# A Mamba-style decoder step: clamping the decay exponents on ScalarE in place of a mask matmul, and a first chunk without a carried state

## The chip, the cores and the metric

The kernel runs on one core of one Trainium2 chip. The metric is the device time of one execution in microseconds (us); the document gives the median of several runs. One core has a matrix engine (TensorE, PE in the profile; its weight loads are listed apart as PEld), a vector engine (VectorE, DVE), an activation engine (ScalarE, ACT), GpSimd (POOL) and a queue that issues most DMAs (SyncE, SP). The engines run their own instruction streams and meet only at semaphores.

## The reference, cut to what matters

One decoder layer is computed for a prompt of 512 tokens and for 8 sample tokens: a combined projection, a state-space (SSD) branch and a pooling branch, cross-attention, an MLP and norms. The change touches only the chunked SSD scan over the prompt, with 4 chunks of 128 tokens, 32 heads in 4 groups, head size 64 and state size 128:

```python
cs = jnp.cumsum(dt * A, axis=2)                       # per chunk and head; A < 0, dt > 0
seg = cs[:, :, :, None] - cs[:, :, None, :]           # l (out token) minus s (in token)
lmat = jnp.exp(jnp.where(causal, seg, -jnp.inf))      # causal: l >= s
cb = jnp.einsum('bclgn,bcsgn->bclsg', Cm, Bm)
y_diag = jnp.einsum('bclsgk,bcsgkp->bclgkp', cb[..., None] * lmat, xdt)
chunk_states = jnp.einsum('bclgn,bclgkp->bcgkpn', Bm, xdt * decay_to_end[..., None])
def step(s, inp):
    dec, st = inp
    return s * dec[..., None, None] + st, s
s_fin, s_prev = lax.scan(step, s0, (chunk_decay, chunk_states))   # s0 = 0 for the prompt
y_off = jnp.einsum('bclgn,bcgkpn->bclgkp', Cm, s_prev) * jnp.exp(cs)[..., None]
y = y_diag + y_off                                    # then + d_skip * xs
```

Since dt is positive and A negative, cs falls along a chunk, so seg is not positive wherever the mask keeps it.

## The kernel before, in words

Every large projection is a run of calls `gemm(t)` over tiles t of 128 output columns: 48 matmuls each (8 slices of the contraction, three products of split float32 operands, two halves of 260 tokens), all on line 376. For each tile ScalarE makes `w_hi` (line 354), VectorE makes `w_lo` (line 361), and the result stays in one of two PSUM slots until it is evacuated.

The SSD scan is woven into these projections. It has 16 steps s = 1 to 16, four chunks c (0 to 3) times four groups gr (0 to 3). TensorE's stream for it is written out in full. For each step it issues:

- `step_a`: the product of B and C (line 1651), a transpose of B (line 1652), and `rows_of_cs` for heads 0 to 3, then the semaphore `cb_ready`.
- tiles of the projection: in chunks 0 and 1 a whole tile of 48 matmuls (none for s = 1), in chunks 2 and 3 half a tile, 24 matmuls.
- `step_b`: it waits for `exp_a` (ScalarE) and `x_prep` (VectorE), then issues `rows_of_cs` for heads 4 to 7, the product of C with the carried state (line 1660) and the new chunk state (line 1661), then `off_ready`.
- another whole tile (chunks 0 and 1) or the second half tile (chunks 2 and 3).
- `step_c`: it waits for `m_ready` (VectorE), then issues the products of the eight decay matrices with the inputs (line 1667), then `y_mm`.

`rows_of_cs` writes a PSUM bank of 4 heads by 128 tokens with two matmuls of 512 columns: line 1644 multiplies a bfloat16 identity by a mask that holds 0 or -1e30, and line 1646 adds the cumulative sums, spread over the partitions.

ScalarE runs two loops of two iterations (lines 745 to 767) with four groups each. For each step it copies `b_tok` and then turns the bank into `decay[:, 0:4]` with four activations (`decays`, line 732: Exp of the row plus a per-partition bias `ncs`, the negated sum), which sets `exp_a`; after `off_ready` it does the same for heads 4 to 7 (`exp_b`). Between these it serves the projection tiles (`split_hi`, line 354, and a tanh or a copy).

VectorE's loops are `prep` (lines 1123 and 1124, the second sets `x_prep`), `weights_a` (line 1129 multiplies C B by the triangle `triu` into `cbm`, line 1131 multiplies `decay[:, 0:4]` by `cbm`), `carry` (line 1136 scales the state's output, lines 1137 and 1139 renew the state, line 1141 multiplies `decay[:, 4:8]` by `cbm` and sets `m_ready`), and `finish_y` (lines 1146 and 1148). In chunks 0 and 1 two projection tiles are served in between (lines 361 and 1153), in chunks 2 and 3 one. GpSimd zeroes the state (line 502), builds the constants at the start (lines 471 to 488) and computes the skip term of each step (line 507).

## Time and profile before

| | us |
|---|---|
| median of three runs | 1327.97 |
| lowest and highest run | 1327.3 and 1332.85 |
| the profiled execution, its time | 1328.24 |
| its span, first to last instruction | 1326.5 |
| TensorE matmul busy in it | 1266.1 (95%) |
| VectorE busy | 760.0 (57%) |
| ScalarE busy | 451.2 (34%) |
| GpSimd busy | 163.9 (12%) |

The span is shorter than the device time by 1.7 us, which lies outside the first and last instruction. All positions in time below are microseconds from the start of the span. The scan's 16 steps lie between 198.5 and 411.7. Busy shares are means over stages with different limits, so what a change is worth must be read from its own stage. The records of matmuls overlap because they are pipelined; the distance between the starts of successive records tells what one costs, not its duration. The mean granted TensorE clock was 0.978 of full speed.

### The profile page before, as it was taken

How to read it: one execution, taken by the hardware profiler on the slowest of the kernel's cores; microseconds unless marked ns; L12 is line 12 of the kernel's file. 1: busy time of each engine (PE TensorE's matmuls, PEld its weight loads, DVE VectorE, ACT ScalarE, POOL GpSimd, SP SyncE). 2: the span in 40 equal slices, each digit the busy share in tenths (PEclk: the TensorE clock that was granted, in tenths of full speed). 3: DMA queues.
4: the chain of work that ended last, by engine and by line, in shares of the span. 5: the costliest groups of instructions: out<-in, count | busy, mean ns of one | idle time of the engine just before them, and what ended most of it. 6: DMA issues, size and time to landing. Idle time of an engine off the chain costs nothing.

```text
span 1326.5 us, 23554 instructions
## 1 busy us (share of the span) xinstructions
PE 1266.1 (95%) x9799; PEld 1190.4 (90%) x9799; DVE 760.0 (57%) x1494; ACT 451.2 (34%) x752; POOL 163.9 (12%) x194
## 2 busy tenths in 40 slices
PE   6999999999998999699999998999999999999996
PEld 5999998998887988699999985459999999999996
DVE  5677866666776656753444457323645765743433
ACT  4444423333332235432245223223431331322422
POOL 1000003000112733200010000001112222200000
PEclk7999999999998999899999997999999999999998
DMA  6423222222124563042234639401645556433211
GB/s 220 120 64 94 73 65 82 73 65 64 33 80 130 144 163 93 32 161 96 88 104 168 214 108 366 161 0 64 206 138 179 176 178 190 144 112 96 96 64 65
DMA packets 141701, 158.15 MB, mean 119 GB/s; under 512 B 4506, under 2 KB 132682, under 8 KB 141169
## 3 DMA queue, kind: packets, MB, share of 16 engines
q1 hardware_dynamic: 135764, 135.37, 32.8%
q0 software_dynamic: 4384, 21.15, 4.8%
q8 instruction: 74, 1.21, 0.4%
q10 hardware_dynamic: 1456, 0.23, 0.1%
q14 instruction: 23, 0.19, 0.0%
HBM read 140.70 MB, written 16.70 MB: 119 GB/s over the span
## 4 chain that ended last, share of the span: by engine, by line
PE 88%; DVE 6%; ACT 2%; issue 1%; DMA 1%; POOL 1%; SPq 0%; DVEq 0%; ACTq 0%
PE slot L376 70%; PE slot L1908 2%; PE slot L1819 2%; PE aux L1667 2%; DVE junk L1412 1%; PE aux L1660 1%; PE aux L1661 1%; PE aux L1881 1%; PE slot L1899 1%; DMA vr<-in_conv_b 1%; DMA w_raw<-in_w_xo 1%; DVE w_lo L361 1%; ACT w_hi L354 1%; PE aux L1644 1%; PE aux L1646 1%
## 5 line engine op out<-in xcount | busy, mean ns | idle before, releaser
L361 DVE TENSOR_TENSOR w_lo<-w_raw,w_hi 128x1024 fp32r<-128x1024 f32 x186 | 249.8, 1343 | 351.7 <-ACT w_hi L354 351.5
L354 ACT ACTIVATE w_hi<-w_raw 128x1024 fp32r<-128x1024 f32 x186 | 196.9, 1059 | 555.8 <-PE slot L376 519.6
L376 PE MATMUL slot<-a_hi,w_hi 128*128 128x260 f32 x1408 | 296.0, 292 | 0.7 <-DVE a_lo L1453 0.7
L376 PE MATMUL slot<-a_hi,w_lo 128*128 128x260 f32 x1408 | 284.5, 284 | 0.0
L376 PE MATMUL slot<-a_lo,w_hi 128*128 128x260 f32 x1408 | 283.9, 283 | 0.0
L376 PEld LDWEIGHTS slot<-a_hi,w_hi 128*128 128x128 f32 x1408 | 221.2, 190 | 12.8 <-issue 9.7
L376 PEld LDWEIGHTS slot<-a_lo,w_hi 128*128 128x128 f32 x1408 | 218.2, 189 | 0.0
L376 PEld LDWEIGHTS slot<-a_hi,w_lo 128*128 128x128 f32 x1408 | 217.9, 189 | 0.0
L376 PE MATMUL slot<-b_hi,w_hi 128*128 128x260 f32 x640 | 129.0, 283 | 1.6 <-DVE gate_b L1281 1.6
L376 PE MATMUL slot<-c_hi,w_hi 128*128 128x260 f32 x640 | 129.4, 283 | 0.2 <-DVE c_lo L1365 0.2
L376 PE MATMUL slot<-b_hi,w_lo 128*128 128x260 f32 x640 | 129.0, 283 | 0.0
L376 PE MATMUL slot<-c_hi,w_lo 128*128 128x260 f32 x640 | 129.0, 283 | 0.0
L376 PE MATMUL slot<-b_lo,w_hi 128*128 128x260 f32 x640 | 128.8, 283 | 0.0
L376 PE MATMUL slot<-c_lo,w_hi 128*128 128x260 f32 x640 | 128.7, 283 | 0.0
L376 PEld LDWEIGHTS slot<-b_hi,w_hi 128*128 128x128 f32 x640 | 98.7, 188 | 1.8 <-issue 1.8
L376 PEld LDWEIGHTS slot<-c_hi,w_hi 128*128 128x128 f32 x640 | 98.7, 189 | 0.4 <-DVE c_lo L1365 0.4
L376 PEld LDWEIGHTS slot<-c_hi,w_lo 128*128 128x128 f32 x640 | 98.7, 188 | 0.0
L376 PEld LDWEIGHTS slot<-b_hi,w_lo 128*128 128x128 f32 x640 | 98.7, 188 | 0.0
L376 PEld LDWEIGHTS slot<-b_lo,w_hi 128*128 128x128 f32 x640 | 98.4, 188 | 0.0
L376 PEld LDWEIGHTS slot<-c_lo,w_hi 128*128 128x128 f32 x640 | 98.4, 188 | 0.0
L1074 DVE SCALAR_TENSOR_TENSOR hbuf<-cbuf,cols,hbuf 128x512 f32<-128x512 f32 x72 | 54.1, 752 | 8.4 <-DVE hbuf L1074 1.1
L1469 DVE SCALAR_TENSOR_TENSOR rt<-slot,rstd 128x520 f32<-128x520 f32 x32 | 22.4, 700 | 57.7 <-PE slot L376 57.7
(402 smaller groups left out, 1596.2 us busy)
## 6 DMA issues: line engine op xcount, KB each, us to landing
w_raw<-in_w_in SPq DMA_DIRECT2D x32, 1024.0 KB, 6.1
w_raw<-in_w_up SPq DMA_DIRECT2D x16, 1024.0 KB, 5.4
w_raw<-in_w_down SPq DMA_DIRECT2D x16, 1024.0 KB, 5.2
sring<-in_state_ssm SPq DMA_DIRECT2D x16, 512.0 KB, 5.4
w_raw<-in_w_ssd_proj SPq DMA_DIRECT2D x8, 1024.0 KB, 5.1
cache<-in_cache_mem_k SPq DMA_DIRECT2D x8, 1024.0 KB, 7.8
cache<-in_cache_mem_v SPq DMA_DIRECT2D x8, 1024.0 KB, 5.0
uring<-in_state_ssm SPq DMA_DIRECT2D x16, 512.0 KB, 4.0
```

The source lines that it names most:

```text
L354: nc.scalar.activation(w_hi[:, t % 2], w_raw[:, t // 2 % 2, :, t % 2 * P:t % 2 * P + P], ACT.Copy).then_inc(hi_ready, 1)
L361: nc.vector.tensor_tensor(w_lo[:, t % 2], w_raw[:, t // 2 % 2, :, t % 2 * P:t % 2 * P + P], w_hi[:, t % 2].bitcast(F32), ALU.subtract).the ...
L376: last = nc.tensor.matmul(slot[t % 2][:, h, 0:HALF], w[:, t % 2, k, :], act[:, k, h * HALF:(h + 1) * HALF], start=(start and k == 0 and n ...
L1074: ins = nc.vector.scalar_tensor_tensor(out=h, in0=b[:, k:k + SEQ], scalar=cols[:, bass.ds(C_CW + CT * k + f, 1)], in1=h, op0=ALU.mult, op1 ...
L1412: ins = nc.vector.tensor_tensor_reduce(junk[:, m, h, :], cache[b % CR][:, m, h * XD:(h + 1) * XD], q_bank(b)[:, h // 2, h % 2 * XD:(h % 2 ...
L1469: nc.vector.scalar_tensor_tensor(out=halves(rt[k % 2][:]), in0=in_slot(t % 2), scalar=0.0, in1=halves(rstd[:]), op0=ALU.max, op1=ALU.mult) ...
L1644: nc.tensor.matmul(aux[:, 0, :], identb[:], maskneg[:].unsqueeze(1).to_broadcast([P, 4, P]), start=True, stop=False)
L1646: return nc.tensor.matmul(aux[:, 0, :], pick_step[:, n:n + 1].to_broadcast([P, P]), cs_rows[:], start=False, stop=True)
L1660: nc.tensor.matmul(aux[:, 2, :], bc[:, GROUPS + gr, c * P:(c + 1) * P], state[:, gr, :], start=True, stop=True)
L1667: last = nc.tensor.matmul(aux[:, 2, j * HD:(j + 1) * HD], decay[:, j, :], xdt[:, j * HD:(j + 1) * HD], start=(j == 0), stop=(j == HPG - 1) ...
L1819: last = nc.tensor.matmul(slot[t % 2][:, 0, 0:MEM], w[:, t % 2, kk, :], u[:, kk, :], start=(kk == 0 and q == 0), stop=(kk == KT - 1 and q ...
L1908: last = nc.tensor.matmul(slot[h // 2][0:NS, 1, h % 2 * XD:(h % 2 + 1) * XD], p_diag[:, m, b, h, :], cache[n % CR][:, m, h * XD:(h + 1) * ...
```

## The change

`rows_of_cs` no longer issues the mask matmul; the spread of the sums is a single matmul. The bank then holds the plain sums cs_l. ScalarE computes Relu(cs_s - cs_l) into `decay` with four activations of 128 columns, waits for them, and takes Exp of the negative of all four heads in one activation of 512 columns in place. Where the mask had made the exponent very negative it is now zero or less and gives at most 1, and the product with `cbm`, which already holds zeros there, removes it. The column of sums is kept with its own sign as `cs_col` in place of `ncs`.

In chunk 0 the product of C with the carried state (line 1660) is left out. VectorE copies the new chunk state into `state` in place of `carry`'s three operations and adds the skip term straight to the product in PSUM in place of `finish_y`'s two. For this VectorE's first loop, of two iterations, is written out in full. The zeroing of `state` and the wait for it go, as do the constants `identb` and `maskneg` with their four GpSimd instructions, so that TensorE waits for three constants at the start in place of five.

```diff
-            nc.gpsimd.memset(identb[:], 0.0)
-            nc.gpsimd.memset(maskneg[:], 0.0)
...
-            nc.gpsimd.affine_select(out=identb[:], in_=identb[:], compare_op=ALU.not_equal, fill=1.0, base=0,
...
-            nc.gpsimd.affine_select(out=maskneg[:], in_=maskneg[:], compare_op=ALU.is_ge, fill=NEG, base=0,
...
-            nc.gpsimd.memset(state[:], 0.0).then_inc(st_zero, 1)
...
             def decays(sem_in, s, c, gr, j0, sem_out):
                 act.wait_ge(sem_in, s)
                 for j in range(j0, j0 + 4):
-                    last = nc.scalar.activation(decay[:, j, :], aux[:, 0, (j - j0) * P:(j - j0 + 1) * P], ACT.Exp,
-                                                bias=ncs[:, c, gr * HPG + j:gr * HPG + j + 1])
-                last.then_inc(sem_out, 1)
+                    last = nc.scalar.activation(decay[:, j, :], aux[:, 0, (j - j0) * P:(j - j0 + 1) * P], ACT.Relu, scale=-1.0,
+                                                bias=cs_col[:, c, gr * HPG + j:gr * HPG + j + 1])
+                chain(last)
+                nc.scalar.activation(decay[:, j0:j0 + 4, :], decay[:, j0:j0 + 4, :], ACT.Exp, scale=-1.0).then_inc(sem_out, 1)
...
-                    chain(nc.vector.tensor_scalar(ncs[:].rearrange(fl), aux[:, 2, 0:P], -1.0, None, ALU.mult))
-                    nc.vector.tensor_tensor(dtd[:].rearrange(fl), aux[:, 2, P:2 * P], ncs[:].rearrange(fl), ALU.add).then_inc(cs_v, 1)
+                    chain(nc.vector.tensor_copy(cs_col[:].rearrange(fl), aux[:, 2, 0:P]))
+                    nc.vector.tensor_tensor(dtd[:].rearrange(fl), aux[:, 2, P:2 * P], cs_col[:].rearrange(fl), ALU.subtract).then_inc(cs_v, 1)
...
+            def first_state(s, gr):
+                dve.wait_ge(off_ready, s)
+                nc.vector.tensor_copy(state[:, gr, :], aux[:, 3, :])
+                dve.wait_ge(exp_b, s)
+                nc.vector.tensor_tensor(decay[:, 4:8, :], decay[:, 4:8, :], cbm[:].unsqueeze(1).to_broadcast([P, 4, P]),
+                                        ALU.mult).then_inc(m_ready, 1)
+
+            def first_y(s, gr):
+                dve.wait_ge(y_mm, s)
+                dve.wait_ge(skip_ready, s)
+                nc.vector.tensor_tensor(xs_tok[:, 0, gr * GW:(gr + 1) * GW], aux[:, 2, :], xskip[:], ALU.add).then_inc(y_ready, 1)
...
-            with dve.Fori(0, 2) as i:
-                chain.loop(i, 12)
+            for c in range(2):
                 for gr in range(GROUPS):
...
+                    if c == 0:
+                        first_state(s, gr)
+                    else:
+                        carry(s, c, gr)
...
-            pe.wait_ge(consts, 5)
+            pe.wait_ge(consts, 3)
...
-                nc.tensor.matmul(aux[:, 0, :], identb[:], maskneg[:].unsqueeze(1).to_broadcast([P, 4, P]), start=True, stop=False)
                 n = 8 * c + 2 * gr + j0 // 4
-                return nc.tensor.matmul(aux[:, 0, :], pick_step[:, n:n + 1].to_broadcast([P, P]), cs_rows[:], start=False, stop=True)
+                return nc.tensor.matmul(aux[:, 0, :], pick_step[:, n:n + 1].to_broadcast([P, P]), cs_rows[:], start=True, stop=True)
...
                 rows_of_cs(c, gr, 4)
-                nc.tensor.matmul(aux[:, 2, :], bc[:, GROUPS + gr, c * P:(c + 1) * P], state[:, gr, :], start=True, stop=True)
+                if c:
+                    nc.tensor.matmul(aux[:, 2, :], bc[:, GROUPS + gr, c * P:(c + 1) * P], state[:, gr, :], start=True, stop=True)
```

## Rows read from the trace of the kernel before

**Rows 1.** The page: busy time by engine.

```profile
PE 1266.1 (95%) x9799; PEld 1190.4 (90%) x9799; DVE 760.0 (57%) x1494; ACT 451.2 (34%) x752; POOL 163.9 (12%) x194
```

**Rows 2.** Busy time by stretch: stretch, length, each engine's busy us, TensorE clock, DMA.

```profile
209.00:317.00 108.00, 108.00 (x815) 99.97 (x814) 67.56 (x93) 37.74 (x87) 8.09 (x7) 1.00 0.25 69
...
331.00:410.00 79.00, 79.00 (x563) 69.86 (x562) 57.52 (x82) 30.64 (x83) 8.37 (x7) 1.00 0.18 47
```

**Rows 3.** Timeline, step_a of s = 10: start, duration, engine, line, operation.

```profile
335.77 0.10 PEld L1644 LDWEIGHTS aux<-maskneg,identb 128*128 128x128 bf16 x1
335.88 0.19 PEld L1646 LDWEIGHTS aux<-cs_rows,pick_step 128*128 128x128 f32 x1
336.10 0.42 PEld L376 LDWEIGHTS slot<-a_hi,w_hi 128*128 128x128 f32 x2
```

**Rows 4.** Timeline of the weight loads, step_b of s = 10.

```profile
339.17 0.10 PEld L1644 LDWEIGHTS aux<-maskneg,identb 128*128 128x128 bf16 x1
...
339.40 0.42 PEld L1660 LDWEIGHTS aux<-state,bc 128*128 128x128 f32 x2
```

**Rows 5.** Timeline of the weight loads, step_a of s = 1.

```profile
198.54 0.30 PEld L1651 LDWEIGHTS aux<-bc 128*128 128x128 f32 x2 [0.98 <-issue]
198.75 0.14 PEld L1652 LDWEIGHTS aux<-ident,bc 128*128 128x128 f32 x1
```

**Rows 6.** Timeline of the matmuls, step_b of s = 9.

```profile
328.55 0.38 PE L1644 MATMUL aux<-maskneg,identb 128*128 128x512 bf16 x1 [0.24 <-DVE xdd L1124]
...
328.99 1.02 PE L1660 MATMUL aux<-state,bc 128*128 128x512 f32 x2
329.84 1.02 PE L1661 MATMUL aux<-xdd,b_tok 128*128 128x512 f32 x2
```

**Rows 7.** Timeline of VectorE: the end of prep for s = 9 and s = 10.

```profile
327.71 0.68 DVE L1124 TENSOR_TENSOR xdd<-xs_tok,dtd 128x512 f32 x1
...
338.08 0.68 DVE L1124 TENSOR_TENSOR xdd<-xs_tok,dtd 128x512 f32 x1
```

**Rows 8.** Timeline of s = 1: ScalarE's decays and TensorE's wait for them.

```profile
199.80 1.14 ACT L732 ACTIVATE decay<-aux,ncs 128x128 f32<-128x128 f32 x4
...
200.99 0.39 PE L1644 MATMUL aux<-maskneg,identb 128*128 128x512 bf16 x1 [1.40 <-ACT decay L732]
```

**Rows 9.** Groups of ScalarE instructions: count, busy us, mean ns, idle before.

```profile
L732 ACT ACTIVATE decay<-aux,ncs 128x128 f32<-128x128 f32 x128 | 36.5, 372 | 36.4 <-PE aux L1661 36.4
...
L692 ACT ACTIVATE tbuf<-hbuf 128x512 f32<-128x512 f32 x24 | 15.2, 633 | 59.4 <-DVE hbuf L1074 59.4
```

**Rows 10.** Timeline of s = 9: decays of heads 4 to 7 up to step_c.

```profile
331.00 1.14 ACT L732 ACTIVATE decay<-aux,ncs 128x128 f32<-128x128 f32 x4 [4.24 <-PE aux L1661]
...
332.92 0.68 DVE L1141 TENSOR_TENSOR decay<-decay,cbm 128x512 f32<-128x512 f32 x1
...
333.66 1.86 PEld L1667 LDWEIGHTS aux<-xdt,decay 128*128 128x128 f32 x16
```

**Rows 11.** Timeline of ScalarE: the last table load before the scan, the first after.

```profile
158.87 1.28 ACT L692 ACT_TABLE_LOAD   x1
...
492.05 1.28 ACT L784 ACT_TABLE_LOAD   x1
```

**Rows 12.** TensorE by stretch: stretch, length, busy us, granted clock, DMA share, GB/s.

```profile
199.50:201.00 1.50, 0.10 (x2) 1.00 1.11 386
...
411.00:412.00 1.00, 0.00 (x0) 0.96 0.00 0
412.00:413.00 1.00, 0.76 (x4) 0.50 0.00 0
```

**Rows 13.** The chain that ended last, in order of time: start, duration, what.

```profile
5.67 9.25 DMA vr<-in_conv_b
...
421.65 7.29 PE slot L376 x48
...
429.81 5.73 PE slot L376 x48
```

More of the change, by code:

```diff
@@ L48 @@
 UW = 256
-NEG = -1.0e30
 F32 = mybir.dt.float32
@@ L226, in build @@
         ident = const("ident", [P, P])
-        identb = const("identb", [P, P], BF16)
         triu = const("triu", [P, P])
         ones = const("ones", [P, P])
-        maskneg = const("maskneg", [P, P], BF16)
         cols = const("cols", [P, 176])
@@ L234, in build @@
         a_row = const("a_row", [P, HEADS])
-        ncs = const("ncs", [P, NCH, HEADS])
+        cs_col = const("cs_col", [P, NCH, HEADS])
         ecs = const("ecs", [P, NCH, HEADS])
@@ L284, in build @@
         off_ready, y_mm, skip_ready, y_ready, tz_ready = (sem(n) for n in ("off_ready", "y_mm", "skip_ready", "y_ready", "tz_ready"))
-        st_zero = sem("st_zero")
         old_in, old_tr, old_ev = sem("old_in"), sem("old_tr"), sem("old_ev")
@@ L745, in _ @@
             with act.Fori(0, 2) as i:
+                chain.loop(i, 8)
                 for gr in range(GROUPS):
@@ L752, in _ @@
                     z_tile(T_Z + 2 * gr + 1, i)
+                chain.end(2)
             act.wait_ge(smp_v, 1)
@@ L757, in _ @@
             with act.Fori(0, 2) as i:
+                chain.loop(i, 8)
                 for gr in range(GROUPS):
@@ L767, in _ @@
                                          ACT.Copy).then_inc(evacuated[t % 2], 1)
+                chain.end(2)
             for k in range(8):
@@ L1158, in _ @@
             dve.wait_ge(spilled, 16)
-            dve.wait_ge(st_zero, 1)
             dve.wait_ge(cs_v, 2)
-            with dve.Fori(0, 2) as i:
-                chain.loop(i, 12)
+            for c in range(2):
                 for gr in range(GROUPS):
-                    s = 4 * i + gr + 1
-                    prep(i, gr)
+                    s = 4 * c + gr + 1
+                    prep(c, gr)
                     weights_a(s)
-                    z_tile(T_Z + 2 * gr, 2 * gr, i)
-                    carry(s, i, gr)
-                    z_tile(T_Z + 2 * gr + 1, 2 * gr + 1, i)
-                    finish_y(s, i, gr)
-                chain.end(2)
+                    z_tile(T_Z + 2 * gr, 2 * gr, c)
+                    if c == 0:
+                        first_state(s, gr)
+                    else:
+                        carry(s, c, gr)
+                    z_tile(T_Z + 2 * gr + 1, 2 * gr + 1, c)
+                    if c == 0:
+                        first_y(s, gr)
+                    else:
+                        finish_y(s, c, gr)
             with dve.Fori(0, 2) as i:
```

2 lines of the change are left out of this document (removed).

## The prediction

> **What bounds the kernel now.** I read the views from the outside in. The page's busy times come first: TensorE is busy 95% of the span and every other engine 57% or less [rows 1]. The means say nothing of the scan, so the busy times by stretch come next. In chunks 0 and 1 (108.00 of 108.00 us) and in chunks 2 and 3 (79.00 of 79.00 us) TensorE has no gap, at full clock, while ScalarE is busy 35% and 39% and VectorE 63% and 73% of the time [rows 2]. So in the scan TensorE's own instruction stream is the path, and an instruction taken from it shortens the kernel by the distance that its record puts between its neighbours, unless a wait behind it takes the time. The timelines of single steps then give those distances and the slack of each wait: `exp_a` and `x_prep` ahead of step_b, `m_ready` ahead of step_c.
>
> **Mask matmul in step_a.** The weights of the next matmul are loaded as the current one starts, so the start of a load marks the start of the matmul before. The load of line 1646 starts at 335.88 and the next one at 336.10: the mask matmul occupies 0.22 us [rows 3]. The float32 load that now has to stand in its place can begin at 335.77, under the transpose of line 1652, and has the 0.11 us until 335.88; in an exposed place two such loads start within 0.21 us, 0.105 each [rows 5]. It fits, so the whole 0.22 is saved. That holds for 14 of 16 steps, s = 2 to 8 and 10 to 16: 14 x 0.22 = 3.1 us. s = 1 and s = 9 follow below.
>
> **Mask matmul in step_b.** Here the load comes behind two waits and starts only as the last matmul of the tile has ended. From 339.17 to 339.40 the pair of a short bfloat16 load and the mask matmul takes 0.23 us [rows 4]. What takes its place is an exposed float32 load, 0.105 us [rows 5] and say 0.11. The saving is 0.23 - 0.11 = 0.12 us, 16 x 0.12 = 1.9 us. The bounds: nothing of the new load hidden, 1.9; all of it hidden, 16 x 0.23 = 3.7. I take the lower, because the row's load did start late.
>
> On this the Trainium skill, page "TensorE: Matmul & The Clock Gate", has two rules. Its section "LDWEIGHTS (loading the stationary operand)" gives columns / 1.2 ns, an estimate of 107 ns for 128 columns, and the section on weight-path modes keeps the fast load from float32 weights; by these the step saves 0.12, as in the sum. Its section "Architectural detail: the array is 16× 32×32, not 1× 128×128" lets loads be pulled ahead of matmuls in flight; by that the step would save 0.23 and the sum would be 1.8 us larger. The load at 339.17, after the tile, does not agree with the second rule in this place.
>
> **State product in chunk 0.** Line 1660 starts at 328.99 and line 1661 at 329.84, so the two passes take 0.85 us [rows 6]. Four are removed: 3.4 us. The load for line 1661 can then go under line 1646, as that of line 1660 did.
>
> **ScalarE's extra activation.** Each call of `decays` had four activations in 1.14 us [rows 8, 10], and keeps them as Relu; I take Relu to cost what Exp did with the same bias operand (372 ns, overlapped) [rows 9]. New are a wait for the last of them and one Exp of 512 columns. The nearest row is the tanh of 128x512 between the same memories, 0.63 us [rows 9]. The wait I put at 0.03 and bound by 0.15. So `exp_a` and `exp_b` come 0.66 us later, at most 0.8. In total ScalarE gets 32 x 0.66 = 21 us more, under the projection tiles in which it idles 60% of the time [rows 2]. Behind the new wait on ScalarE stand `split_hi` and the tanh or copy of the next tile. In s = 9, a half-tile step, `decays` ended at 332.14 and TensorE was busy until 333.6 with the tile that `split_hi` waits for anyway, so 0.8 us fits.
>
> Where does the 0.66 touch TensorE?
> - s = 1: there is no tile between step_a and step_b, and TensorE waited 1.40 us for `exp_a`, until 200.99 [rows 8]. The bank is now ready 0.22 earlier, so the Relus run from 199.58 to 200.72, the Exp ends at 201.38, and with the 0.05 us of handover of before (200.94 to 200.99) TensorE goes on at 201.43: 0.44 us lost, step_a's saving included.
> - Chunks 2 and 3, heads 4 to 7, eight times: `exp_b` was ready at 332.14 but VectorE, busy with carry, started line 1141 only at 332.92 [rows 10]. New: 332.14 + 0.03 + 0.63 + 0.05 = 332.85. It is hidden by carry with 0.07 us to spare. Without that cover it would delay `m_ready`, which is already last: line 1141 ended at 333.60 and step_c's first load came at 333.66 [rows 10]. I count nothing; the bounds are 0 and 8 x 0.15 = 1.2 us lost.
> - Chunks 0 and 1: a whole tile of 5.73 us stands between [rows 13], so nothing.
>
> **x_prep, the next wait.** TensorE reaches step_b of chunks 2 and 3 0.22 us earlier. In s = 10 line 1124 ended at 338.76 and the load came at 339.17, now at 338.95; in s = 9, where TensorE really waited, line 1124 ended at 328.39 and the matmul came at 328.55, 0.16 later [rows 4, 6, 7]. So 338.92 against 338.95: just free. VectorE's chain up to there hangs on the end of the tile, not on the mask, and does not move. In s = 9 the wait exists already and swallows step_a's 0.22, which is why it is not among the 14.
>
> **VectorE, GpSimd, start.** In chunk 0 VectorE does one copy for three operations and one addition for two, 3 operations of some 0.7 us less, as line 1141 [rows 10], in each of four steps. It is not the path there: nothing. In chunks 0 and 1 TensorE waits for it nowhere but at s = 1, so writing out the loop costs nothing either. Copy for multiply and subtract for add in the preparation of the sums is of equal size. GpSimd's four constants bring TensorE's start forward by under 1 us, but the chain runs through a DMA of conv_b from 5.67 to 14.92 [rows 13]: nothing. The zeroing of `state` is beside the path.
>
> **The sum.** 3.1 + 1.9 + 3.4 - 0.4 = 8.0 us. From the profiled execution's own 1328.24 us (span 1326.5 and 1.7 around it, both kept) that is 1320.2 us. That execution is 0.3 us above the median of the runs, 1327.97, which is too little to matter. 8.0 us is 0.60%; a change under 0.5%, 6.6 us, cannot be told from none.
>
> **The rivals.**
> - *The clock falls at s = 1* (chance 0.17). TensorE's idle time there grows from 1.40 to 1.40 + 0.22 + 0.44 = 2.06 us. For: after a microsecond without any matmul (411 to 412) the granted clock went from 0.96 to 0.50, the 1.2 GHz level [rows 12]. Against: at 199.5 to 201.0 TensorE did 0.10 us of work in 1.50 and the clock stayed at 1.00 [rows 12]. The price from the fall near 421: a tile took 7.29 us where the next but one took 5.73, 1.6 us [rows 13]. Time 1321.8.
> - *ScalarE or VectorE becomes last in chunks 2 and 3* (0.12). The margins are 0.07 us at `exp_b` and 0.03 us at `x_prep`. If either is missed by 0.1 to 0.3 us in each of eight steps, 0.8 to 2.4 us go: 1321.0 to 1322.6. For: the smallness of the margins, and that `m_ready` ends last there now. Against: both come out positive.
> - *The load is hidden in step_b too* (0.10): 16 x 0.11 = 1.8 us more gain, 1318.4.
> - *Slower: Relu does not share ScalarE's table with Exp* (0.03). Then each `decays` has a table load ahead of Relu and one ahead of Exp, 1.28 us each [rows 11]. At `exp_b` in chunks 2 and 3 that is 2.56 - 0.07 = 2.5 us for each of eight steps, 20 us, and 2.6 at s = 1: 1320.2 + 22.6 = 1342.8 or more. The point from which it decides is a delay of 8.0 / 8 = 1.0 us in each of those steps. Against: Copy, Exp and Tanh take turns through the whole scan without a load (none lies between 158.87 and 492.05) [rows 11]; but Relu is not among them, so the trace leaves it open. The Trainium skill, page "ScalarE: Activation LUTs", section "Table sets: the hidden batching unit", says that cheap functions, relu and copy named, are in every set and that tanh is in the set of exp; for the latter pair the trace agrees, for relu no run yet shows it.
> - *The gain is lost elsewhere* (0.03): a later stage waits for something that hangs on absolute time. The weight loads hang on TensorE's own progress, so I see no such place. 1325 to 1328.
>
> **How the numbers follow.** The forecast keeps 0.55, and its own range is 1319.2 to 1321.2. Taking in the clock's fall, the missed margins and the hidden load, with half a microsecond for the scatter of medians, gives 1317.6 to 1324.0; outside stay the table loads, the loss elsewhere and the tails. Faster by over 0.5% (under 1321.3): most of the forecast (0.51), the hidden load (0.10), and a third to a half of the two cases near 1322 (0.10), 0.71 together. Slower: 0.04. The same: the rest, 0.25.
>
> **What would show it.** In the changed kernel's profile: in step_a the load for line 376 starts 0.11 us after that for line 1646, where 0.33 lay between the mask's load and it [rows 3]. Chunk 0 takes 3.4 + 3 x 0.22 + 4 x 0.12 - 0.44 = 4.1 us less, chunk 1 takes 4 x 0.34 = 1.4 less, chunks 2 and 3 together 7 x 0.34 + 0.12 = 2.5 less. TensorE's wait before the first step_b ends at `exp_a` and is about 2.1 us long. ScalarE shows 32 activations of 128x512 of about 0.63 us, with no table load between Relu and Exp. In chunks 2 and 3 line 1141 still starts 1.92 us after the first activation of heads 4 to 7, as from 331.00 to 332.92 [rows 10]. The prediction is wrong if step_b's distances do not shrink, if `m_ready` comes later than that, or if the granted clock just behind s = 1's step_b is below 1.

## The result

| | us |
|---|---|
| before, first comparison | 1330.41 (1327.3 to 1336.03, 4 executions) |
| after, first comparison | 1317.3 (1316.86 to 1319.65, 4 executions) |
| ratio | 0.9893, 95% interval 0.9869 to 0.9916 |
| ratio, repeated later (6 executions of after, 15 of before) | 0.9921, 0.9901 to 0.9941 |
| span of the profiled execution | 1315.5, against 1326.5 before |

The changed kernel is faster, by 13.1 us in the first medians and by 11.0 us between the two profiled executions. The forecast was 1320.2 us with a range of 1317.6 to 1324.0, so the sign held and the size did not: the measured median lies 0.3 us below the range. One term of the sum, the mask matmul in step_b, was too small by 1.3 us; the rest of the miss is scatter, as the last part works out.

Executions of either kernel fall into clusters up to some 5 us apart (before near 1327.5 and 1332.3, after near 1317 and 1322), and four executions of each do not mix them equally. Why is told with the first and the ninth experiment.

The page after the change shows where the work went: TensorE has 12.4 us less than in [rows 1], ScalarE 19.7 us more, VectorE 6 us less.

```profile
PE 1253.7 (95%) x9759; PEld 1181.7 (90%) x9759; DVE 754.0 (57%) x1482; ACT 470.9 (36%) x784; POOL 159.1 (12%) x189
```

Step_a of s = 10, weight loads. The load of line 376 (now 372) starts 0.11 us after the spread's, where [rows 3] had 0.33 from the mask's load on. This term was right.

```profile
328.78 0.19 PEld L1654 LDWEIGHTS aux<-cs_rows,pick_step 128*128 128x128 f32 x1
328.89 0.42 PEld L372 LDWEIGHTS slot<-a_hi,w_hi 128*128 128x128 f32 x2
```

Step_b, first in chunk 0 (s = 3). The last two loads of the tile are the pair at 215.48, the second 0.12 later at 215.60. The spread's float32 load starts 0.11 after it and its matmul at 215.83, as the next load shows. The load is not exposed at all.

```profile
215.48 0.31 PEld L372 LDWEIGHTS slot<-a_hi,w_lo 128*128 128x128 f32 x2
215.71 0.19 PEld L1654 LDWEIGHTS aux<-cs_rows,pick_step 128*128 128x128 f32 x1
215.83 0.42 PEld L1670 LDWEIGHTS aux<-xdd,b_tok 128*128 128x128 f32 x2
```

The same place before the change (s = 2). The mask's load is recorded at 217.25, 0.24 after the tile's last load, and its matmul starts in the same hundredth: in this place the record of the bfloat16 load sits directly at its matmul, and says nothing of the earliest moment at which a float32 load could start. (In step_a it does not sit there: in [rows 3] the same load starts at 335.77, 0.11 us ahead of its matmul.)

```profile
216.89 0.31 PEld L376 LDWEIGHTS slot<-a_hi,w_lo 128*128 128x128 f32 x2
217.25 0.10 PEld L1644 LDWEIGHTS aux<-maskneg,identb 128*128 128x128 bf16 x1
217.25 0.20 PEld L1646 LDWEIGHTS aux<-cs_rows,pick_step 128*128 128x128 f32 x1
217.48 0.42 PEld L1660 LDWEIGHTS aux<-state,bc 128*128 128x128 f32 x2
```

Chunks 2 and 3, step_b of s = 10. Line 1118 (before: 1124) ends at 331.77 and the load follows 0.12 us later, the distance at which TensorE had waited for it in s = 9 before (328.39 to the weight load at 328.51; the matmul record is in [rows 6]). So `x_prep` now comes just as it is needed. It costs nothing yet: the tile's last load starts at 331.73 and the spread's matmul at 331.97, 0.24 us later, as in chunk 0 (215.60 and 215.83), where line 1118 ends 3.0 us ahead of the load.

```profile
331.09 0.68 DVE L1118 TENSOR_TENSOR xdd<-xs_tok,dtd 128x512 f32 x1
...
331.61 0.31 PEld L372 LDWEIGHTS slot<-a_hi,w_lo 128*128 128x128 f32 x2
331.89 0.18 PEld L1654 LDWEIGHTS aux<-cs_rows,pick_step 128*128 128x128 f32 x1
332.00 0.42 PEld L1669 LDWEIGHTS aux<-state,bc 128*128 128x128 f32 x2
```

ScalarE and VectorE in s = 9, answering [rows 10]. The Exp ends at 325.81, and line 1135 (before: 1141) starts at 325.93, 1.92 us after the first activation, exactly as before.

```profile
324.01 1.14 ACT L721 ACTIVATE decay<-aux,cs_col 128x128 f32<-128x128 f32 x4 [3.65 <-PE aux L1670]
325.18 0.63 ACT L724 ACTIVATE decay<-decay 128x512 f32<-128x512 f32 x1
...
325.93 0.69 DVE L1135 TENSOR_TENSOR decay<-decay,cbm 128x512 f32<-128x512 f32 x1
```

At s = 1 TensorE waits 2.06 us, against 1.40 in [rows 8]:

```profile
200.76 0.51 PE L1654 MATMUL aux<-cs_rows,pick_step 128*128 128x512 f32 x1 [2.06 <-ACT decay L724]
```

The groups of ScalarE instructions give the two prices that the trace before could not show: Relu costs what Exp did in [rows 9], and the Exp of 512 columns costs what the tanh did.

```profile
L721 ACT ACTIVATE decay<-aux,cs_col 128x128 f32<-128x128 f32 x128 | 36.4, 372 | 26.0 <-PE aux L1670 25.8
...
L724 ACT ACTIVATE decay<-decay 128x512 f32<-128x512 f32 x32 | 20.3, 633 | 1.0
```

There is no table load between these rows of ScalarE's timeline, one on each side of the scan as in [rows 11]:

```profile
158.18 1.28 ACT L681 ACT_TABLE_LOAD   x1
...
481.35 1.28 ACT L778 ACT_TABLE_LOAD   x1
```

**Where the time went.** The yardstick of the experiments is the distance between the first weight loads of successive step_c's, read from the timeline of weight loads. It hardly depends on the clock's moods, since the granted clock is 1.00 from the first step_c to the last in all fourteen profiles.

```
                     s1 to s16   each of chunk 0   chunk 1   s8 to s9   each of chunks 2, 3
before                 199.56      16.23-16.28     16.24-16.27  11.09     10.65-10.70
after                  190.75      14.94-14.98     15.79-15.83  10.95     10.21-10.26
```

(The interval from s = 4 to s = 5 is the first of chunk 1.) In the seven steps s = 10 to 16 the saving is 0.43 us on average, 0.21 in step_a and 0.22 in step_b. In s = 9, where TensorE waits for `x_prep` in both kernels, it is 0.14, all of it in step_b. Between the two profiled executions the 11.0 us divide so: start-up until the first transposes of `abuf` 0.6 (42.04 to 41.41); from there to the first scan load nothing (156.50 and 156.45); from there to the first step_c 0.5 (10.26 and 9.73); the scan 8.8; from the last step_c's end to line 1716 0.9, which is the clock (below); the rest nothing. The change itself accounts for 0.5 + 8.8 = 9.3 us.

### The profile page after: what moved, and what is told of

Its sections match the earlier page's. It is cut to its first block, busy times and chain, and to the rows that moved or that the text cites. A ratio compares the mean times of both kernels' runs of the same rounds, so it can differ in the third digit from the quotient of the medians.

```text
span 1315.5 us, 23400 instructions
## 1 busy us (share of the span) xinstructions
PE 1253.7 (95%) x9759; PEld 1181.7 (90%) x9759; DVE 754.0 (57%) x1482; ACT 470.9 (36%) x784; POOL 159.1 (12%) x189
## 4 chain that ended last, share of the span: by engine, by line
PE 87%; DVE 6%; ACT 2%; issue 1%; DMA 1%; POOL 1%; SPq 0%; DVEq 0%; ACTq 0%
PE slot L372 71%; PE slot L1917 2%; PE slot L1828 2%; PE aux L1676 2%; DVE junk L1421 1%; PE aux L1670 1%; PE aux L1890 1%; PE slot L1908 1%; PE aux L1669 1%; DMA w_raw<-in_w_xo 1%; ACT w_hi L350 1%; DVE w_lo L357 1%; DMA vr<-in_conv_b 1%; PE aux L1654 1%; PE aux L1578 1%
## 5 line engine op out<-in xcount | busy, mean ns | idle before, releaser
L372 PEld LDWEIGHTS slot<-a_hi,w_hi 128*128 128x128 f32 x1408 | 221.2, 190 | 12.4 <-issue 9.7
```

The costliest lines, as they stand in the source:

```text
L372: last = nc.tensor.matmul(slot[t % 2][:, h, 0:HALF], w[:, t % 2, k, :], act[:, k, h * HALF:(h + 1) * HALF], start=(start and k == 0 and n ...
```

## The experiments

**1. The changed kernel again.** No edit.

> The changed kernel itself, unedited. The profiles of before and after differ by 11.0 us of span, the medians of the first runs by 13.1, with two runs of before at 1332.85 and 1336.03 that pull its median up. Theory A (the gain is some 10 us and the rest is scatter of the kernel before): ratio 0.990 to 0.993. Rival B (a gain of 13 us or more that the two profiled executions do not show in full): ratio 0.989 or less. In this profile: the distance from the first weight load of the first step_c to that of the last is 190.75 us, as in the first profile of after (199.56 before); the start of the first scan matmul may move by some 0.7 us either way if the start-up gain was chance.

Measured: 1321.84 us (1316.3 to 1322.45, 6 executions), ratio 0.9921, 0.9901 to 0.9941. The profiled execution has a span of 1319.6, 4.1 us more than the first one of the same kernel, and the scan distance is 190.71. Theory A holds: the interval centres on 10.5 us and ends short of rival B. (The two medians, 1330.41 and 1321.84, are 8.6 us apart, also within it.) The added time lies ahead of the first step_c. From the first `abuf` transposes to the first scan load it takes 159.68 in place of 156.45, and from there to step_c 11.16 in place of 9.73. The windows of TensorE (stretch, length, busy us and count, granted clock, DMA share, GB/s) show the reason, for the first profile of the changed kernel and for this one:

```profile
180.00:184.00 4.00, 4.00 (x30) 0.78 0.25 83
184.00:188.00 4.00, 4.00 (x28) 0.79 0.00 0
188.00:192.00 4.00, 4.00 (x36) 1.00 0.00 0
...
204.00:208.00 4.00, 4.00 (x37) 1.00 0.02 4
```

```profile
180.00:184.00 4.00, 4.00 (x20) 0.50 0.23 83
184.00:188.00 4.00, 4.00 (x20) 0.50 0.02 4
188.00:192.00 4.00, 4.00 (x28) 0.75 0.00 0
...
204.00:208.00 4.00, 3.99 (x15) 0.62 0.02 6
```

In this execution TensorE ran at 1.2 GHz (0.50) for some ten us, from just behind the start of the 32 narrow matmuls of line 1640 on, and again behind its wait at s = 1. In the first it ran so for a few us, once, from the end of the narrow matmuls on. The prediction had named a granted clock below 1 just behind s = 1 as a sign that it is wrong; here it is 0.62. Experiment 9 finds the same fall in the kernel before, so that sign does not tell the two kernels apart.

**2. The mask matmul alone.** The changed kernel with chunk 0 computed as before.

```diff
-                if c:
+                if True:
                     nc.tensor.matmul(aux[:, 2, :], bc[:, GROUPS + gr, c * P:(c + 1) * P], state[:, gr, :], start=True, stop=True)
...
-                    if c == 0:
-                        first_state(s, gr)
-                    else:
-                        carry(s, c, gr)
+                    carry(s, c, gr)
```

(Likewise `finish_y`, and the zeroing of `state` with its wait is back.)

> The mask matmul goes as in the changed kernel, but chunk 0 is computed as before, with the product of the zeroed state, carry and the two additions. Theory A (the float32 load of the spread is hidden in step_b, so each mask matmul is worth its whole 0.22 to 0.23 us): first step_c to last step_c is 6.3 us shorter than before (199.56 to 193.2), and the device time 6 to 7 us less. Rival of the prediction (load exposed, 0.12 saved in step_b): 4.8 us shorter. At s = 1 TensorE's wait for the Exp costs 0.44 us in both.

Measured: scan distance 193.35, 6.2 us less than before; device time 1325.51 (1320.41 to 1328.72), ratio 0.9955, 0.9937 to 0.9974. Each step of chunks 0 and 1 is 15.79 to 15.83, 0.44 less. That is 0.22 in step_a and 0.22 in step_b, and Theory A. The prediction's 0.34 per step is refuted. (The first step_c comes late here, 11.93 us after the first scan load, because the clock fell at s = 1; the scan distance does not contain that.)

**3. The first chunk alone.** The kernel before with `first_state`, `first_y`, the written-out loop and `if c:` ahead of line 1660.

> Only chunk 0 is changed (no state product, copy in place of carry, one addition, VectorE's first loop written out); mask matmul and ScalarE as before. The prediction's term: 4 x 0.85 = 3.4 us less, of it 2.55 between the first and the last step_c (199.56 to 197.0). Rival (VectorE's shorter work or the written-out loop gives something too): more than 3.6 us and shorter waits of TensorE for VectorE.

Measured: 1324.75 us (1323.7 to 1328.48), ratio 0.9953, 0.9935 to 0.9971. The three steps of chunk 0 take 15.37, 15.41 and 15.42, so 0.89, 0.82 and 0.86 less than before: 2.57 us in all, 0.85 each. The prediction's term holds to the hundredth, and VectorE's shorter work gave nothing. The whole distance is 197.21, 2.35 less, because the steps of chunks 2 and 3 took 10.70 here where half of them took 10.65 before; two executions of the same program differ as much (199.56 and 199.75, experiment 9). The device times stand 5.7 us apart in the medians and 6.3 (3.9 to 8.6) by the ratio, more than the predicted 3.4 and even more than the rival's 3.6. The profile shows 3.2 from the first scan load to the last step_c, and the shorter waits that the rival asks for are not there; the rest is put down to the scatter between executions that experiment 9 describes, which was not shown for these executions one by one.

**4. The constants put back.** Only GpSimd's part of the start is restored:

```diff
+            nc.gpsimd.memset(identb[:], 0.0)
...
+            nc.gpsimd.memset(maskneg[:], 0.0)
...
+            nc.gpsimd.affine_select(out=identb[:], in_=identb[:], compare_op=ALU.not_equal, fill=1.0, base=0,
+                                    pattern=[[-1, P]], channel_multiplier=1).then_inc(consts, 1)
...
-            pe.wait_ge(consts, 3)
+            pe.wait_ge(consts, 5)
```

> The changed kernel with the four GpSimd instructions that built identb and maskneg put back, and TensorE waiting for five constants again; nothing uses the two tiles. Theory A (the earlier start of the scan by 0.68 us was chance, set by when the conv_b DMA landed and when the clock rose): same time as the changed kernel within 1 us, and its DMA of conv_b lands between 14.4 and 15.0 us. Rival (the shorter constants set is worth 0.7 us): 0.7 us slower than the changed kernel in every part behind the start, with conv_b landing at 14.9 again.

Measured: 1322.63 us (1317.25 to 1323.31), ratio 0.9935, 0.992 to 0.995, and a profiled span of 1315.5, that of the changed kernel. The first `abuf` transposes come at 41.43 with the constants and at 41.41 and 41.43 without. The DMA of conv_b lands at 14.53, within the range of theory A. The start-up gain of 0.6 us was therefore chance. Over all profiles this moment lies anywhere from 40.32 to 42.69, in no order with the constants.

**5. ScalarE's part alone.** The kernel before with the new `decays` and `cs_col`; the mask matmul stays.

> The kernel before with ScalarE's part of the change alone: four Relu, a wait, one Exp of 512 columns, the mask matmul still there (the masked entries become 1e30, whose Exp of the negative is 0). Prediction: 0.65 us lost at s = 1 (TensorE's wait 1.40 to 2.05) and nothing elsewhere, because carry hides it in chunks 2 and 3 by 0.07 us: first to last step_c stays at 199.56. Rival (the margin is missed): that distance grows by 0.1 us or more for each of 8 steps, 0.8 us or more in all.

Measured: ratio 0.9998, 0.9984 to 1.0011 (1332.18 against 1331.93 us). Scan distance 199.62 against 199.56: the Exp of 512 columns is hidden in all 15 steps behind s = 1, margins of a tenth of a microsecond or less included. TensorE's wait at s = 1 is 2.07 us, 0.67 more than in [rows 8], as expected. That 0.7 us is below what the ratio can show. `m_ready` does end last in chunks 2 and 3, as the prediction said, but it hangs on VectorE's own chain and not on the Exp.

```profile
204.85 0.61 PE L1649 MATMUL aux<-maskneg,identb 128*128 128x512 bf16 x1 [2.07 <-ACT decay L735]
```

**6. The spread matmul twice.**

```diff
+                nc.tensor.matmul(aux[:, 0, :], pick_step[:, n:n + 1].to_broadcast([P, P]), cs_rows[:], start=True, stop=True)
                 return nc.tensor.matmul(aux[:, 0, :], pick_step[:, n:n + 1].to_broadcast([P, P]), cs_rows[:], start=True, stop=True)
```

> The changed kernel with the spread matmul issued twice in a row in every call, the second overwriting the first: a matmul as long as the mask's, but with a float32 weight load. Theory A (a float32 load is hidden behind the last matmul of the tile in step_b): first to last step_c grows from 190.75 by 15 x 0.22 in step_a (less what the x_prep wait swallows in s = 9) and 15 x 0.22 in step_b, 6.3 us in all, to 197.0 or 197.1, just as the mask matmul cost. Rival (the bfloat16 load was what was exposed, so that the mask cost more than its matmul): growth of 4.8 us or less.

Measured: scan distance 197.62, 6.9 us more than the changed kernel; device time 1329.59 (1322.51 to 1332.6), ratio 0.9976, 0.9957 to 0.9996. A matmul of 512 columns with a float32 load costs 0.24 us a call (6.9 over 29 calls; at s = 9 the wait for `x_prep` swallows step_a's), slightly more than the mask did with its bfloat16 load. The rival, a growth of 4.8 us or less, is out. The steps s = 10 to 16 grow by 0.48 us, as much as those of chunks 0 and 1 (0.47). If TensorE had lost anything to `x_prep` there in the changed kernel, part of the growth would have gone into that wait. In the timeline of the weight loads of step_b (chunk 0) the first load again starts 0.12 before its matmul, and the matmul takes 0.24:

```profile
237.89 0.19 PEld L1654 LDWEIGHTS aux<-cs_rows,pick_step 128*128 128x128 f32 x1
238.01 0.19 PEld L1655 LDWEIGHTS aux<-cs_rows,pick_step 128*128 128x128 f32 x1
238.25 0.42 PEld L1671 LDWEIGHTS aux<-xdd,b_tok 128*128 128x128 f32 x2
```

**7. Half a tile in the wait at s = 1.**

```diff
                         if s > 1:
                             gemm(pe, T_Z + 8 * c + 2 * gr, a_hi, a_lo)
-                        step_b(c, gr, s)
-                        gemm(pe, T_Z + 8 * c + 2 * gr + 1, a_hi, a_lo)
+                            step_b(c, gr, s)
+                            gemm(pe, T_Z + 8 * c + 2 * gr + 1, a_hi, a_lo)
+                        else:
+                            gemm(pe, T_Z + 1, a_hi, a_lo, kts=range(0, 4))
+                            step_b(c, gr, s)
+                            gemm(pe, T_Z + 1, a_hi, a_lo, kts=range(4, 8))
```

> The changed kernel, but the first half (24 matmuls) of the projection tile behind step_b of s = 1 is issued ahead of it, so that TensorE has 2.9 us of work while ScalarE makes exp_a. Theory (the 2.06 us wait is all that the longer ScalarE chain costs, and it can be filled): 2.0 us faster than the changed kernel, wait before the first step_b gone, first to last step_c unchanged at 190.75 or up to 0.2 longer. Rival (the wait moves to m_ready of s = 1, since only 24 matmuls are left behind step_b for VectorE's copy and product): TensorE waits 0.5 us or more before the first step_c and the gain is 1.5 us or less.

Measured: 1318.64 us (1314.1 to 1320.46), ratio 0.9894, 0.987 to 0.9918. From the first scan load to the first step_c it takes 7.54 us in place of 9.73 (11.16 where the clock fell): 2.2 us less, and the scan distance stays at 190.80. The rival's new wait is there, but small: VectorE waits 0.41 us for the Exp and ends at 208.21, and step_c's load comes at 208.26, 0.25 us behind the tile's last load (208.02) where 0.12 is the distance without a wait. That is 0.13 us, not the 0.5 that the rival asked for.

```profile
206.85 0.64 ACT L724 ACTIVATE decay<-decay 128x512 f32<-128x512 f32 x1
...
207.52 0.69 DVE L1142 TENSOR_TENSOR decay<-decay,cbm 128x512 f32<-128x512 f32 x1 [0.41 <-ACT decay L724]
...
208.26 0.52 PEld L1676 LDWEIGHTS aux<-xdt,decay 128*128 128x128 f32 x4
```

**8. xdd made early, and VectorE's last loop written out.** `x_prep` did two jobs: it told that xdd was ready, and that VectorE had read the last product from the PSUM bank that step_b writes. The second goes to `y_ready`.

```diff
+            def prep_state(c, gr):
+                ...
+                nc.vector.tensor_tensor(heads(xdd[:]), xs, dtd[:, c, hd].unsqueeze(2).to_broadcast([P, HPG, HD]),
+                                        ALU.mult).then_inc(xdd_ready, 1)
...
                     carry(s, c, gr)
+                    if s < 16:
+                        prep_state(s // GROUPS, s % GROUPS)
...
-                pe.wait_ge(x_prep, s)
+                pe.wait_ge(xdd_ready, s)
+                if s > 1:
+                    pe.wait_ge(y_ready, s - 1)
```

> The changed kernel with VectorE making xdd for the next step right behind m_ready, in its idle time, under a semaphore of its own; step_b waits for that, and for the last step's y_ready, in place of x_prep. VectorE's last loop is written out. Theory (x_prep is the wait that ends last before step_b in chunks 2 and 3, each load following line 1118's end by 0.12 us): s = 9 gains 0.3 us or more and each of the seven steps behind it up to 0.1, 0.4 to 1.0 us between first and last step_c. Rival (it is not x_prep but exp_a or TensorE's own stream): no change within 0.1 us, or exp_a is named as the releaser.

Measured: scan distance 189.49, 1.26 us less than the changed kernel and above the 1.0 of the theory. s = 9 takes 10.18 in place of 10.95, the seven behind it 10.16 to 10.18 in place of 10.21 to 10.26, and the chunks ahead do not move. Device time 1319.83 (1314.64 to 1322.84), ratio 0.9915, 0.9891 to 0.9939.

Of s = 9, 0.70 us lies between step_a and step_b (4.15 to 3.45 between their first loads): that is `x_prep`, a wait that the kernel before had too. The 0.06 or 0.07 us that each of the eight steps gains besides does not lie there. In s = 11 to 16 the distance from step_a to step_b is 3.41 to 3.45 in the changed kernel and 3.44 to 3.45 here, and in s = 10 the spread's load starts 0.12 us after the tile's last (329.81) where it was 0.16 (331.73 and 331.89), but its matmul comes 0.24 us after that load in both:

```profile
329.69 0.31 PEld L372 LDWEIGHTS slot<-a_hi,w_lo 128*128 128x128 f32 x2
329.93 0.19 PEld L1660 LDWEIGHTS aux<-cs_rows,pick_step 128*128 128x128 f32 x1
330.06 0.42 PEld L1677 LDWEIGHTS aux<-state,bc 128*128 128x128 f32 x2
```

That gain lies ahead of step_c, at `m_ready`. Here are VectorE's first operation of `carry`, its last one and step_c's load in s = 10, in the changed kernel and then in this one:

```profile
334.23 0.69 DVE L1130 TENSOR_TENSOR yacc<-aux,ecs 128x512 f32<-128x512 f32 x1 [0.69 <-PE aux L1670]
...
336.16 0.68 DVE L1135 TENSOR_TENSOR decay<-decay,cbm 128x512 f32<-128x512 f32 x1
336.46 0.31 PEld L372 LDWEIGHTS slot<-a_hi,w_lo 128*128 128x128 f32 x2
336.90 1.86 PEld L1676 LDWEIGHTS aux<-xdt,decay 128*128 128x128 f32 x16
```

```profile
332.20 0.69 DVE L1134 TENSOR_TENSOR yacc<-aux,ecs 128x512 f32<-128x512 f32 x1 [1.15 <-PE aux L1678]
...
334.13 0.69 DVE L1139 TENSOR_TENSOR decay<-decay,cbm 128x512 f32<-128x512 f32 x1
334.52 0.31 PEld L372 LDWEIGHTS slot<-a_hi,w_lo 128*128 128x128 f32 x2
334.88 1.86 PEld L1684 LDWEIGHTS aux<-xdt,decay 128*128 128x128 f32 x16
```

Step_c's load follows the end of VectorE's last operation by 0.05 us in both. It comes 0.32 us behind the tile's last load in the changed kernel, in the kernel before likewise (s = 9 to 16), and 0.24 here; in chunks 0 and 1, without a wait, it is 0.12. So TensorE waits 0.20 us for `m_ready` in each of the eight steps, before and after the change, and 0.12 here. The gain comes from the start of `carry`: 0.72 us after the start of the state product's last pass in every one of these steps in the eleven profiles whose last loop is a loop, and 0.63 in the three (experiments 8, 11 and 12) where it is written out. The first step shows the same pair where xdd is not made early: 0.72 in experiment 5 (loop) and 0.63 in experiment 2 (written out). The experiment thus changed two things, and only the 0.70 us of s = 9 belong to the early xdd. The theory that `x_prep` was the wait that ends last is right for s = 9 and not for the seven steps behind it.

**9. The kernel before again.** No edit.

> The kernel before, unedited, for a second profile. Its executions lie near 1327.5 or near 1332.3 us, those of the changed kernel near 1317.2 or near 1322.2. Theory (the five us are one longer stretch at the 1.2 GHz level behind the 32 narrow matmuls at 179 to 183 us, which either kernel has or has not): if this execution takes over 1331, its granted clock is 0.50 from about 181 to 189 and the distance from those narrow matmuls to the first scan matmul is 3 us longer than the 18.9 of the first profile; the scan from first to last step_c is 199.6 in any case. Rival (the scatter lies elsewhere, in DMA waits or at the end): a slow execution with the same 18.9 us there.

Measured: 1332.45 us, span 1330.7, scan distance 199.75. The theory holds for the stretch behind the narrow matmuls (3.2 us longer); it had not foreseen the second fall, at s = 1. TensorE's windows:

```profile
180.00:184.00 4.00, 4.00 (x23) 0.59 0.48 167
184.00:188.00 4.00, 4.00 (x21) 0.50 0.01 4
188.00:192.00 4.00, 4.00 (x24) 0.63 0.00 0
...
204.00:208.00 4.00, 3.60 (x7) 0.58 0.19 65
```

From the first `abuf` transposes to the first scan load it takes 159.67, as in experiment 1, against 156.50 in the first profile; from there to the first step_c 11.94 against 10.26. So the kernel before also has the clock's fall at s = 1 in such executions, with its wait of only 1.40 us. The two kernels stand 11.0 us apart (1326.5 and 1315.5) and 11.1 apart (1330.7 and 1319.6). Of the 11.1, 9.8 lie between the first scan load and the last step_c, 0.85 ahead of the `abuf` transposes and 0.5 behind the scan.

All fourteen profiles together say more. From the `abuf` transposes to the first scan load those that wait ahead of the narrow matmuls need 156.4 to 156.5 us, 157.9 to 158.1, or 159.6 to 159.7, with a stretch at 0.50 of about 3, 7 or 10 us: there are three lengths, not two. In the five with the longest (experiments 1, 2, 5, 6 and 9, both kernels among them) the clock falls 0.5 to 1.2 us after the first narrow matmul has started, in the others 1.4 us or more after it. The fall at s = 1 is in those five profiles and in none of the six others that wait there, whether the wait is 1.40 or 2.06 us. So in these profiles it goes with the longer stretch before it and not with the wait that the change made longer.

**10. Half a tile ahead of the narrow matmuls.**

```diff
             for t in range(17, 24):
-                gemm(pe, t, a_hi, a_lo)
+                gemm(pe, t, a_hi, a_lo, kts=range(4 if t == 23 else 0, KT))
+                if t == 22:
+                    gemm(pe, 23, a_hi, a_lo, kts=range(0, 4))
```

> The changed kernel, but the first half (24 matmuls) of projection tile 23 is issued ahead of the 32 narrow matmuls, where TensorE waits 1.6 us for ScalarE, and the other half behind them. Theory (that wait with the narrow matmuls behind it is what lets the clock fall, sometimes for 3 and sometimes for 10 us): 1.6 us faster from the wait, and the fall behind it shorter or gone, so up to 5 us faster in the median and less scatter between executions. Rival (the fall comes from the narrow matmuls alone or from the phase of something else): 1.6 us faster and the two groups of times, 5 us apart, stay.

Measured: 1317.63 us (1316.08 to 1319.69), ratio 0.9901, 0.9883 to 0.9918. In the profile the wait is gone: 154.72 from the `abuf` transposes to the scan, 1.7 less than 156.45. The clock still falls to 0.50 at the end of the narrow matmuls (0.61 over 184 to 188). No execution of six reached the 1322 of the changed kernel, near which five of six lay in experiment 1. The theory fits, but six executions do not prove that the long fall is gone.

**11. Experiments 7 and 8 together.**

> The changed kernel with both edits that took out a wait: half a tile ahead of step_b of s = 1, and xdd of the next step made early on VectorE. Theory (independent waits): the sum, 2.2 us before the first step_c and 1.3 us between first and last, 3.5 us faster than the changed kernel, and no clock fall at s = 1. Rival (one uncovers the other, the wait for m_ready moves in): 2.5 us or less.

Measured: 1316.02 us median of six executions (lowest 1313.89; one of 1556.59, with a mean granted clock of 0.744 where the others have 0.974 to 0.979, stands alone and is unexplained), ratio 0.9888, 0.9867 to 0.9909. In the profile 7.55 us to the first step_c and a scan of 189.59: both gains in full, 2.2 and 1.2 us, and independent. There is no clock fall at s = 1, but this execution had the middle stretch (158.1), with which none was seen in experiment 3 either, whose wait stands.

**12. All three.**

> All three edits together: half of tile 23 ahead of the narrow matmuls, half a tile ahead of step_b of s = 1, xdd early. Theory: 3.5 + 1.6 = 5.1 us faster than the changed kernel, and more if the clock fall behind the narrow matmuls is shortened too, ratio to the kernel before 0.985 to 0.989. Rival (the fall moves to another place, such as the 402 to 425 stretch): less than 4 us.

Measured: 1313.2 us (1312.66 to 1315.39, 4 executions), ratio 0.9864, 0.9843 to 0.9885, and the scan distance 189.49. The ratio is in the range of the theory. In the profile the three parts add up to 5.2 us: 156.34 against the 158.0 of the same stretch length, 2.2 and 1.3. The kernel did not run side by side with the changed one, so the gain over it is not measured as a time. It is the best of these kernels, 18 us under the kernel before. In its profiled execution the clock stayed at 0.50 longer than in experiment 10 (0.63 over 188 to 192), so the fall is not removed, only made cheaper or rarer.

## Why the prediction was wrong in size

- **Mask matmul in step_a**: right, 0.22 us a step.
- **Mask matmul in step_b**: this is the step that failed. It took 0.12 us, on the ground that "the row's load did start late". Measured: 0.22 in chunks 0 and 1 (experiment 2) and 0.22 in s = 10 to 16. A load's record shows when it started, not when it could have. The bfloat16 load started as its matmul did; the float32 load in its place is 0.11 to 0.12 us ahead of its matmul, under the tile's last matmul. The price of an exposed load was right where TensorE really waits ahead of step_b: 0.12 at s = 1, 0.14 at s = 9. The missed term is 7 x 0.10 + 7 x 0.09 = 1.3 us, and 8.0 + 1.3 is the 9.3 that the change gave. The rival with the load hidden, given 0.10, was the one that came, in fourteen of its sixteen steps and for 1.3 of its 1.8 us. The pull-ahead of weight loads that the Trainium skill states ("TensorE: Matmul & The Clock Gate", "Architectural detail: the array is 16× 32×32, not 1× 128×128") agrees with the load at 215.71, and it was wrongly set aside on one row.
- **State product in chunk 0**: right, 0.85 us (experiment 3).
- **ScalarE's extra activation**: right in every number. Four Relu took 1.14 us, the wait 0.02 to 0.03, the Exp 0.63; nothing was lost in chunks 2 and 3 (experiment 5), and s = 1 lost about what was forecast (2.06 us of waiting; 0.53 us net gain up to step_c with the state product and the mask's 0.12 in it, which is 0.85 + 0.12 - 0.44).
- **x_prep, the next wait**: right. It came out "just free" by 0.03 us, and in s = 10 to 16 it costs nothing that the distance from step_a to step_b shows (experiments 6 and 8). The margin was worked out for a load that starts with the tile's end; for the load that starts 0.12 us earlier it is used up, and the load now follows the end of line 1118 by 0.12 us in three of these seven steps. s = 9 swallowed step_a's saving as forecast and gained 0.14 in all (experiment 8 gives back 0.70 of that wait).
- **m_ready**: right that it is last in chunks 2 and 3. It costs 0.20 us a step in both kernels. Since VectorE's chain up to it starts at the end of step_b, it moved ahead with step_b and took nothing of the saving.
- **VectorE, GpSimd, start**: right; the constants are worth nothing (experiment 4).
- **The clock falls at s = 1**: the fall is real and its price of 1.6 us was near (1.4 to 1.7), but it is not what the longer wait brings: it happens in the kernel before too (experiment 9).
- **The range** allowed "half a microsecond for the scatter of medians", and it is this that put the median outside. With the missed 1.3 us the sum would have given 1328.24 - 9.3 = 1318.9, inside the range of 1317.6 to 1324.0. The profiled execution is 1.7 us under that, of which 0.6 is a start-up that is chance (experiment 4) and 0.9 the clock's fall behind the scan, at 412 before, that this execution lacks. The clock's falls from 180 to 192 and at s = 1 move an execution by up to 5 us more. The front table already had a run of 1332.85 beside 1327.3; the range should have been widened for it. The first comparison's four executions of the changed kernel all lay at 1319.65 or below; the next six had a median of 1321.84, inside the range. That the number fell outside is thus in part luck; that the sum was 1.3 us short is not.
- **Table loads**: none, as the rival's counter-argument had it. The Trainium skill ("ScalarE: Activation LUTs", "Table sets: the hidden batching unit") states that relu is in every set. For the set with Exp and Tanh the trace now agrees (128 Relu and 32 Exp without a load); for the other sets no run here shows it.

What stays open: the repeated comparison gives 10.5 us (0.9921 of 1330.4), with 7.8 to 13.2 in its interval, which holds the forecast 8.0 as well; the two pairs of profiles give 11, and the scan with its lead-in accounts for 9.3. The rest lies within the scatter of the start-up (40.32 to 42.69) and of the clock behind the scan, and was not pursued. What decides which of the clusters an execution falls into is not known, and it was not made to order.

## What to carry to other kernels

Where TensorE was the path here, an inserted matmul of 512 columns cost 0.22 to 0.24 us, and its weight load was free wherever another matmul ran ahead of it; behind a real wait the load showed. Do not price a load from the moment at which its record starts, but from a place where the same kind of load stands behind the same kind of matmul. Removing TensorE work brings a wait nearer by that much if its producer's chain starts ahead of the work removed (`x_prep`), and leaves it where it was if the chain starts behind it (`m_ready`), so list the margins of all waits and what each hangs on. When an edit also changes something else, as the loop of experiment 8, look in the trace for the place where the time went before naming the cause. Before putting a range on a few microseconds, look for stretches of lowered clock in more than one execution of the kernel before: here they outweighed every unknown of the sum.

## What the runs showed of the hardware beyond that

- Behind a tile, a bfloat16 weight load of 128 columns is recorded at the start of its own matmul (217.25 and 217.25) where a float32 load in the same place is recorded 0.12 us ahead (215.71 and 215.83). Behind the transpose of step_a the bfloat16 load too is 0.11 us ahead [rows 3]. Why the two places differ was not tested.
- VectorE starts the first operation behind `off_ready` 0.09 us later when it stands in a loop than when the loop is written out (0.72 and 0.63 us, experiment 8). In the changed kernel's trace a register operation on VectorE for the same source line ends 0.05 us before it (334.19 and 334.23); there is none in experiment 8.
- Within or at the end of the 32 matmuls of 17 columns the granted clock falls to 1.2 GHz in all fourteen profiles, with the wait of 1.6 us ahead of them or without it (experiments 10 and 12), but stays there for very different times in one and the same kernel (0.78 and 0.79 of full clock in 180 to 184 and 184 to 188 in one execution, 0.50 and 0.50 in another). An idle stretch of 1.4 us leaves it at 1.00 in one execution [rows 12] and is followed by 0.58 in another (experiment 9).
- At the end of the scan TensorE idles 1.9 us in both kernels. In the first profile before, the clock fell at 412 [rows 12]; in the first profile after, it did not, which alone made 0.9 us:

```profile
401.00:402.00 1.00, 0.00 (x0) 1.00 0.00 0
402.00:404.00 2.00, 1.78 (x16) 1.00 0.00 0
```
